# Where the sums, factors and applications of the last two k chunks stand in a hybrid decoder's instruction order

## What is computed

```python
x = x + 0.5 * swiglu(rms_norm(x, ...), ...)
h = rms_norm(x, mix_norm[l])
(dq, dk, dv, iq, ik, iw, gq, gk, gv, gz, ga, gb, mq) = split_columns(h @ w_in[l])
out_a = dsa_attention(...)                      # top-k by an indexer, 6 heads
# gated DeltaNet: q, k and v pass a causal conv of width 4 and a silu, then
qh = l2_norm(heads(q)) * HEAD_DIM ** -0.5
kh = l2_norm(heads(k))                          # l2_norm: x * rsqrt(sum(x*x) + EPS), per head of 64
o  = gated_delta_rule_chunked(qh, kh, vh, g, beta)
o  = rms_norm(o, out_gain) * silu(heads(z))
# cross-attention into 256 memory tokens
mem_kv = rms_norm(mem, mem_norm[l]) @ w_mem_kv[l]   # mk (keys), mv (values); keys get a per-head rms_norm
out_c  = memory_attention(mq, mem_kv, ...)
x = x + concat(out_a, out_b, out_c) @ w_out[l]
x = x + 0.5 * swiglu(rms_norm(x, ...), ...)
```

## Time and profile before

| | |
|---|---|
| runs | 2112.2, 2112.43, 2112.84 us |
| the profiled execution | 2112.39 us, span of the profile 2110.6 us |
| TensorE busy | 2084.5 us, 99% of the span |
| VectorE, ScalarE, GpSimd busy | 1034.0, 775.9 and 393.9 us |
| granted TensorE clock | full speed on average |
| DMA | 192.41 MB, mean 91 GB/s |

### The profile page before, as it was taken

The page is one execution under the profiler, slowest core; times in us unless marked ns, Lnnn a source line. Parts: engine busy times, 40 slices in busy tenths (PEclk is TensorE's granted clock), DMA queues, the critical chain, the costliest instruction groups (busy, mean ns, idle before and its releaser), DMA issues.

```text
span 2110.6 us, 31901 instructions
## 1 busy us (share of the span) xinstructions
PE 2084.5 (99%) x13097; PEld 1676.8 (79%) x13097; DVE 1034.0 (49%) x1421; ACT 775.9 (37%) x1096; POOL 393.9 (19%) x373
## 2 busy tenths in 40 slices
PE   9999999999999999999999999999999999999999
PEld 7888888877766888888888888887777668888887
DVE  5433333688766533433333433336887665334322
ACT  5222222475546422222232222224755554222211
POOL 1110011105035501101111110121051355111000
PEclk9999999999999999999999999999999999999999
DMA  5222222322111222222222222223212112222222
GB/s 194 87 96 99 95 90 95 127 84 72 47 69 38 100 99 99 99 95 90 95 100 99 99 99 93 93 103 113 80 62 92 41 41 100 99 99 86 94 105 75
DMA packets 30646, 192.41 MB, mean 91 GB/s; under 512 B 3216, under 2 KB 5392, under 8 KB 11984
## 3 DMA queue, kind: packets, MB, share of 16 engines
q1 hardware_dynamic: 30160, 189.80, 25.8%
q10 hardware_dynamic: 384, 1.14, 0.1%
HBM read 188.70 MB, written 2.10 MB: 90 GB/s over the span
## 4 chain that ended last, share of the span: by engine, by line
PE 85%; DVE 8%; ACT 4%; issue 2%; POOL 1%; DMA 0%; SPq 0%; DVEq 0%; ACTq 0%; POOLq 0%
PE psum L932 27%; PE psum L934 26%; PE psum L933 26%; DVE wl L1838 1%; PE psum L1384 1%; PE psum L1395 1%; ACT wh L1463 1%; PE psum L1248 1%; PE psum L1245 1%; PE psum L1359 1%; DVE acc L1921 1%; POOL comb L892 1%; DVE wrk L1936 1%; DVE XL L1853 1%; DVE m L1934 1%
## 5 line engine op out<-in xcount | busy, mean ns | idle before, releaser
L932 PE MATMUL psum<-XH,wh 128*128 128x512 f32 x1904 | 756.3, 397 | 4.9 <-DVE XL L1798 2.2
L933 PE MATMUL psum<-XL,wh 128*128 128x512 f32 x1904 | 741.9, 390 | 0.0
L934 PE MATMUL psum<-XH,wl 128*128 128x512 f32 x1904 | 741.8, 390 | 0.0
L932 PEld LDWEIGHTS psum<-XH,wh 128*128 128x128 f32 x1904 | 357.2, 188 | 103.2 <-issue 24.7
L934 PEld LDWEIGHTS psum<-XH,wl 128*128 128x128 f32 x1904 | 357.4, 188 | 75.6
L933 PEld LDWEIGHTS psum<-XL,wh 128*128 128x128 f32 x1904 | 357.6, 188 | 70.5 <-issue 1.0
L1846 DVE TENSOR_TENSOR wl<-raw,wh 128x2048 fp32r<-128x2048 f32 x88 | 201.7, 2292 | 159.4 <-ACT wh L1468 159.4
L932 PE MATMUL psum<-HH,wh 128*128 128x512 f32 x704 | 273.9, 389 | 0.0
L933 PE MATMUL psum<-HL,wh 128*128 128x512 f32 x704 | 273.9, 389 | 0.0
L934 PE MATMUL psum<-HH,wl 128*128 128x512 f32 x704 | 273.9, 389 | 0.0
L1463 ACT ACTIVATE wh<-raw 128x2048 fp32r<-128x2048 f32 (+1 forms) x84 | 157.3, 1872 | 305.5 <-PE psum L934 305.5
(11 more groups left out here) (255 smaller groups left out, 1980.1 us busy)
## 6 DMA issues: line engine op xcount, KB each, us to landing
raw<-weights SPq DMA_DIRECT2D x143, 1024.0 KB, 4.8
raw<-weights SPq DMA_DIRECT2D x32, 896.0 KB, 4.4
xT<-xt SPq DMA_DIRECT2D x4, 512.0 KB, 6.3
memT<-memt SPq DMA_DIRECT2D x2, 1024.0 KB, 4.9
out<-xT SPq DMA_DIRECT2D x8, 256.0 KB, 6.0
stripsA<-strip_table SPq DMA_DIRECT2D x2, 768.0 KB, 6.6
raw<-weights SPq DMA_DIRECT2D x2, 512.0 KB, 6.6
stripsB<-strip_table SPq DMA_DIRECT2D x2, 512.0 KB, 7.0
```

The lines of the kernel that those rows point to most:

```text
L932: pe.matmul(out_ap, a_hi, b_hi, start=first, stop=False)
L933: pe.matmul(out_ap, a_hi, b_lo, start=False, stop=False)
L934: return pe.matmul(out_ap, a_lo, b_hi, start=False, stop=last)
```

## The change

The step `factors(2)` stands behind `mm gz 2` instead of behind `ev mk 1`. Nothing else is changed.

```diff
     norm("sq", *pairs(2))
     put(("idx", 5))
     mm("gz", 2)
+    factors(2)
     ev("gz", 2)
     put("silu_vz")
     sel(2)
@@
     ev("mk", 0)
     mm("mk", 1)
     ev("mk", 1)
-    factors(2)
     norm("sq", *pairs(3))
     sel(2)
     mm("mv", 0)
```

## The result

The changed kernel takes 2119.94 us (median of 7 runs, 2118.97 to 2121.43) against 2112.53 for the kernel before (7 runs, 2112.2 to 2113.38). The ratio is 1.0036, 95% interval 1.0025 to 1.0047: 7.4 us slower, where 4.35 were forecast. By this one execution the loss can be read place by place.

The account below looks back on a forecast made before the run. The tensor engine was taken as the bound, busy 2084.5 of 2110.6 us. A loss of 2.1 to 2.25 us per layer, twice, middle 4.35, added to 2112.43 gave 2116.8 us; range 2114.8 to 2118.4.

Parts of the forecast that it names:

- The new wait: In front of mv 0, whose first product waits for the copy of mk 0: about 2.1 us in each layer.
- chain of six distances: Measured distances between steps, from the moved sums to the copy of mk 0, done at 477.58 us, 2.6 us late.
- From there to the sums of mk: Restart 0.15 us and mv products 5.65 us after the copy: memory key sums at 483.38 against 481.17, 2.2 us later.
- The clock falls: Behind the new wait, the 48 mv products at half clock cost 5.65 us more per layer: 2128.1 us; chance 0.03.
- The sum: Waits and restart add 2.1 to 2.25 us per layer, 4.35 over two layers: 2116.8 us, clock unchanged.
- third rival: Clock falls behind the wait in front of mv 0: 11.3 us more than the forecast, 2128.1 us; chance 0.03.
- Everything stands 2.15 to 2.2 us later: After the memory key sums, all engine queues shift by 2.15 to 2.2 us, in each of two layers.
- Rival (1): Not slower: the wait for the mk 0 copy is absent or made up later, 2111.4 or 2112.4 us; chance 0.09.
- Rival (2): A second wait, at mq 0 for unit 10's low part or at mv 0's weight load: 2118.8 us; chance 0.05.

Follow-up runs that it names:

- the run with the filled wait: The changed kernel plus 8 unused matmuls of 512 columns in front of mv 0, where the tensor engine would wait: 2115.98 us, ratio 1.0017.
- two otherwise sound versions: Kernel before with the last k factors behind unit 9, or inside gz 2, selection rounds laid out anew: 2112.33 and 2112.43 us against 2112.77.

## Why the prediction was wrong

*The new wait: right.* The chain of six distances held to 0.02 us: with the 0.28 us of lead taken off, the forecast had the factor at 468.39, the high part at 470.89, the low part at 472.84 and the copy at 476.89; the trace has 468.39, 470.89, 472.82 and 476.88. The wait at mk 1 was given as 0.5 and is 0.41 in the rows, that at mv 0 about 2.1 and is 1.92. The rows count from the modelled end of the product before; by the starts and 0.12 us for that product the second is 2.08.

*From there to the sums of mk: the size was off by a little.* 2.2 us were forecast, 2.37 is what the run with the filled wait shows at unit 11. In the change the first product of mv stood 0.19 us before the second, and the sums of mk began 0.21 behind the last, where the sum had 0.12 for each: 0.16 us.

*"The clock falls": this is the step that failed.* The sum gave the clock behind the new wait no term. Its fall stood as the third rival with a chance of 0.03, on the ground that the clock was 1.00 in every stretch read. The stretch read with a wait in it held one of 1.51 us, so it said nothing on one of 1.92. In the profiled execution the granted clock fell to 0.81 to 0.85 in windows of 5 us, which cost 1.55 us in the first layer and 1.4 in the second. The rival's price was wrong too: 5.65 us had all 48 products at half the clock, and 16 were. An unread row of the trace of before had a wait of 2.17 us at 8.38 us with the clock intact; it would have misled as well, as the same wait in another execution shows.

*"Everything stands 2.15 to 2.2 us later": a term was missing.* The low part of unit 11 was taken as 2.29 us because it had that length before. Before, it started 0.1 us before the end of one of GpSimd's products; where it started well inside one, it took 2.8 to 2.9. That is 0.5 us per layer, shown by its return to 2.29 when GpSimd is held back.

*The sum.* 2.37 + 1.55 + 0.5 is 4.4 in the first layer, and the two layers come to 8.9 in the profiled execution. The filled wait took the clock's and GpSimd's part away and left 2115.98, which is 4.0 us below the median of the change. The forecast had the right sign and the right place, but only the first term. The range ended at 2118.4 because the clock's fall had next to no weight and GpSimd's part none. For the 7.4 us of the medians there is no trace: the profiled execution had a fall in both layers, and how often the others had one isn't known.

*Rival (1)* is out: in the change nothing was made up of what the wait had cost. Only the run with the filled wait made up 1 us, in the inversion stage of the first layer. *Rival (2)*, unit 10's low part late for mq 0, was not seen in the change, and came out as soon as the wait for mk 0 was taken away (0.70 us).

## What to carry to other kernels

A step moved ahead on one engine is paid by what stands behind it on all others: here a copy that had 0.7 us of cover was pushed back by 3.3. Price the wait of the tensor engine with its clock as well, here about 1.5 us for a fall, and give that case a real chance. One wait of that length with the clock intact is no proof: at 2.2 us these traces have both outcomes. Where the wait can't be avoided, work of no use in it can be cheaper than the wait (4.0 us here). An instruction that reads two operands beside a busy GpSimd has no fixed length; look at what was running when it started before taking the length along.

## What was not expected of the hardware

Behind waits of 0.92 and 1.19 us the granted clock stayed 1.00; behind 1.92 (with 0.41 shortly before) it fell in both layers; behind 2.19 it fell in one layer and not in the other of the same execution, and behind 2.17 us at the start of the kernel it fell in one execution and not in another. Eight useless matmuls in the wait of each layer made the kernel 4.0 us faster. By the traces some 3 of them are the clock (1.55 and 1.4) and 1 is GpSimd's collision, gone with the other timing.

A collision between VectorE and GpSimd cost 0.5 us or nothing for the same two instructions, by a shift of less than a microsecond between them. In two otherwise sound versions it took up the whole 0.5 to 0.6 us by which the low part of unit 11 started sooner; with the collision removed from one of them, a gain could still not be told.
